# Cached pages of a paged latent attention: joined key and score products, value products turned round, rope scores in two row strips

## What is computed

```python
def mla_keys(c, w_uk, kn_g):
    return rms_norm(jnp.einsum('blc,chd->blhd', c, w_uk), kn_g)
def mla_scores(q_nope, q_rope, k_nope, kr):
    s = (jnp.einsum('bqhd,bkhd->bhqk', q_nope, k_nope) + jnp.einsum('bqhr,bkr->bhqk', q_rope, kr))
    return s * (MLA_QK ** -0.5)
# per page: c = lat_cache[layer, pages]; kr_p = kr_cache[layer, pages]
#   s = mla_scores(q_nope, q_rope, mla_keys(c, ...), kr_p)      8 heads x 8 queries per sample
#   p = exp(s - m);  l += sum(p);  acc += einsum('bhqk,bkc->bhqc', p, c)
# then the 8 new tokens themselves, and o = einsum('bhqc,chv->bqhv', acc / l, w_uv)
```

## Time and profile before

| what | us |
|---|---|
| three runs of the kernel | 1559.74, 1566.42, 1617.56 (median 1566.42) |
| the profiled execution | 1566.49 |
| its span, first to last instruction | 1564.8 |
| TensorE matmul busy in the span | 1498.6 (96%) |
| VectorE busy | 738.9 (47%) |
| ScalarE busy | 461.5 (29%) |
| GpSimd busy | 258.7 (17%) |
| granted TensorE clock, mean | 0.966 |

### The profile page before, as it was taken

One profiled execution on the slowest core, in us unless ns is written; L12 is line 12 of the kernel. 1 busy time (PEld: TensorE's weight loads), 2 busy tenths in 40 slices (PEclk: granted clock), 3 DMA queues, 4 the chain that ended last, 5 costly groups with the idle time before them and its releaser, 6 DMA issues.

```text
span 1564.8 us, 19947 instructions
## 1 busy us (share of the span) xinstructions
PE 1498.6 (96%) x6400; PEld 1039.4 (66%) x6400; DVE 738.9 (47%) x1446; ACT 461.5 (29%) x1013; POOL 258.7 (17%) x494
## 2 busy tenths in 40 slices
PE   7988889999998999999999888899999999999999
PEld 5656646666776777777766566566668667777776
DVE  1345658888514444430014466688883254444200
ACT  1236335545214111110012363454541141111100
POOL 2000244332022000001100002443320220000000
PEclk9999889999989999999999998899998899999999
DMA  6430424333035334333443204333320354333332
GB/s 247 121 98 0 186 87 120 105 93 104 1 121 167 121 122 123 122 103 123 149 134 112 82 33 170 96 116 100 106 75 28 118 170 121 121 124 122 113 111 94
DMA packets 83626, 174.46 MB, mean 111 GB/s; under 512 B 12641, under 2 KB 51074, under 8 KB 82626
## 3 DMA queue, kind: packets, MB, share of 16 engines
q1 hardware_dynamic: 73872, 163.55, 32.6%
q0 software_dynamic: 9504, 9.19, 2.0%
q10 hardware_dynamic: 146, 0.44, 0.1%
HBM read 166.84 MB, written 6.29 MB: 111 GB/s over the span
## 4 chain that ended last, share of the span: by engine, by line
PE 87%; DVE 7%; ACT 3%; issue 2%; POOL 1%; DMA 1%; SPq 0%; DVEq 0%
PE bank L444 35%; PE bank L786 14%; PE bank L1018 12%; PE bank L887 4%; PE bank L817 4%; PE bank L790 3%; PE bank L793 2%; PE bank L864 1%; ACT area L1574 1%; ACT area L1566 1%; PE bank L673 1%; PE bank L530 1%; POOL xg L1917 1%; PE bank L1003 1%; PE bank L479 1%
## 5 line engine op out<-in xcount | busy, mean ns | idle before, releaser
L444 PE MATMUL bank<-xg,slot 128*128 128x320 f32 x2048 | 558.6, 434 | 9.5 <-DMA slot<-in_weights 9.0
L444 PEld LDWEIGHTS bank<-xg,slot 128*128 128x128 f32 x2048 | 389.1, 190 | 174.4 <-DMA slot<-in_weights 9.0
L1782 ACT ACTIVATE sq<-bank 128x512 f32<-128x512 f32 x256 | 151.8, 593 | 172.4 <-PE bank L786 165.7
L1374 DVE TENSOR_REDUCE small<-sq 128x8 f32<-128x512 f32 x256 | 169.3, 682 | 63.4 <-ACT sq L1782 61.0
L1018 PE MATMUL bank<-area,slot 128*128 128x320 f32 x704 | 189.8, 432 | 0.0
L1018 PEld LDWEIGHTS bank<-area,slot 128*128 128x128 f32 x704 | 133.8, 190 | 55.7
L1930 POOL DMA_DIRECT2D krT<-in_cache_r x256 | 127.7, 499 | 226.9 <-issue 221.1
L1574 ACT ACTIVATE area<-area 128x336 f32<-128x336 f32 (+4 forms) x112 | 63.3, 567 | 334.1 <-DVE area L1523 300.8
L786 PE MATMUL bank<-wuk_nat,area 128*128 128x512 f32 x320 | 145.3, 597 | 0.0
L1466 DVE TENSOR_TENSOR x<-x,bank 128x320 f32<-128x320 f32 x48 | 23.4, 488 | 253.6 <-PE bank L1018 174.8
L1917 POOL TENSOR_SCALAR xg<-x,par 128x320 f32<-128x320 f32 x48 | 58.5, 1226 | 272.4 <-DVE x L1466 266.6
(11 more groups left out here) (324 smaller groups left out, 1746.8 us busy)
## 6 DMA issues: line engine op xcount, KB each, us to landing
slot<-in_weights SPq DMA_DIRECT2D x216, 512.0 KB, 3.6
area<-in_cache SPq DMA_DIRECT2D x160, 128.0 KB, 2.1
kept<-in_cache SPq DMA_DIRECT2D x96, 128.0 KB, 2.1
slot<-in_weights SPq DMA_DIRECT2D x18, 384.0 KB, 4.2
krT<-in_cache_r POOLq DMA_DIRECT2D x256, 16.0 KB, 2.0
xg<-in_ssd_t SPq DMA_DIRECT2D x2, 1024.0 KB, 4.7
area<-in_ssd_n SPq DMA_DIRECT2D x2, 1024.0 KB, 13.4
hs_out<-area POOLq DMA_DIRECT2D x2, 1024.0 KB, 4.1
```

The lines of the kernel that those rows point to most:

```text
L444: last = mm(out[:, 0:T], w[:, k, :], xg[:, k, :], start=(k == 0), stop=(k == KD - 1))
L1374: dve.tensor_reduce(ssk[:, t % 2, 8 * j:8 * j + 8], ksq[k % 3], AX.X, ALU.add).then_inc(V.fire(on["k_summed"]), 1)
L1782: f(ksq[k % 3], b[:, :].rearrange("p (h d) -> p h d", h=HEADS), ACT.Square).then_inc(A.free("key", l, t, j), 1)
```

## The change

- **Key and score products joined.** `wkq` holds, per head, 64 columns of the key weights with 8 query columns on each side, one side for even and one for odd samples. A page is multiplied with two halves of 4 heads x 72 columns (288 each), into two banks next to each other (`pair`, three pairs made of banks 0 to 5). A pair is freed by ScalarE's square. The separate score products are gone. GpSimd copies a sample's query columns into `wkq`.
- **Scores leave through ScalarE.** Per page ScalarE copies 64 columns into `score`, and per group 256 rope columns into `rope_sc`; VectorE then multiplies and adds in SBUF.
- **Rope scores in two strips.** Instead of one product with 128 rows and 256 columns there are two with 64 rows and 128 columns, one for each bank of the last page's pair.
- **Values turned round.** The probabilities are the weights (64 columns) and a page with a column of ones behind it moves through (129 columns). Even pages go to output rows 0 to 63, odd ones to 64 to 127. The column of ones gives the sum, so VectorE's sum and the product with ones are gone. ScalarE copies the result out (`cache_evict`), and TensorE adds the two halves and turns them back with two products of a folding matrix (`cache_fold`), one group later.
- **Rings.** What used the ring "mix" in this stage now uses the banks 6 and 7 ("late"). Behind the last group the prompt work waits until the last square is done, and one output tile of L864 is moved behind the last values.
- **Pages** are 260 numbers a row instead of 256. 

```diff
-PAGE_COLS = 2 * P
+PAGE_COLS = 2 * P + 4
...
-        self.t = [ctx.enter_context(nc.psum_tensor(f"bank{b}", [P, 512], F32)) for b in range(8)]
+        self.pair = [ctx.enter_context(nc.psum_tensor(f"pair{i}", [P, 1024], F32)) for i in range(3)]
+        self.t = [self.pair[b // 2][:, 512 * (b % 2):512 * (b % 2) + 512] for b in range(6)]
+        self.t += [ctx.enter_context(nc.psum_tensor(f"bank{b}", [P, 512], F32)) for b in (6, 7)]
...
-        wuk_nat = sb("wuk_nat", 512)
+        wkq = sb("wkq", 640)[:].rearrange("p (h c) -> p h c", h=HEADS)
...
+        rope_sc = [sq_t[:, 2048 + 256 * i:2304 + 256 * i] for i in range(2)]
+        pacc = [view(7778 + 132 * i, 132) for i in range(2)]
...
@@ TensorE: cache_group
-                for j in range(4):
-                    b = banks.open("proj", "key", l, t, j)
-                    pe.wait_ge(*banks.before("key", l, t, j))
-                    mm(b[:, :], pgroup[i][:, j, 0:P], wuk_nat[:, :], **F).then_inc(banks.full("key", l, t, j), 1)
-                b = banks.open("score", "sc", l, t)
-                pe.wait_ge(*banks.before("sc", l, t))
-                for j in range(4):
-                    mm(b[:, 64 * j:64 * j + 64], pgroup[i][:, j, 0:P], qt[:, :, NQ * s:NQ * s + NQ], **F)
-                n = l * NB * GROUPS + t
-                pe.wait_ge(krT_here[n % KR_GROUPS], 64 * (n // KR_GROUPS + 1))
-                mm(b[:, TP:2 * TP], krT[n % KR_GROUPS][:, :], qrep[:, :, :, NQ * s:NQ * s + NQ]
-                   .rearrange("p j h q -> p (j h) q"), **F).then_inc(banks.full("sc", l, t), 1)
+                at = 8 * (s % 2)
+                if g == 0:
+                    pe.wait_ge(*on["q_slot"].at(l, s + 1))
+                for j in range(4):
+                    k = 4 * t + j
+                    pair = banks.pair[k % 3]
+                    if k >= 3:
+                        pe.wait_ge(*on["key_free"].at(l, k - 2))
+                    else:
+                        pe.wait_ge(*banks.drained(2 * k))
+                        pe.wait_ge(*banks.drained(2 * k + 1))
+                    page = pgroup[i][:, j, 0:P]
+                    mm(pair[:, 0:288], page, wkq[:, 0:4, at:at + 72], **F)
+                    last = mm(pair[:, 512:800], page, wkq[:, 4:8, at:at + 72], **F)
+                    if j == 3:
+                        n = l * NB * GROUPS + t
+                        pe.wait_ge(krT_here[n % KR_GROUPS], 64 * (n // KR_GROUPS + 1))
+                        for half in range(2):
+                            rows = slice(64 * half, 64 * half + 64)
+                            last = mm(pair[:, 512 * half + 288:512 * half + 416], krT[n % KR_GROUPS][rows, :],
+                                      qrep[rows, 2 * half:2 * half + 2, :, NQ * s:NQ * s + NQ]
+                                      .rearrange("p j h q -> p (j h) q"), **F)
+                    last.then_inc(on["key_full"].sem, 1)
...
@@ TensorE: cache_values
-                for j in range(PAGES):
-                    i = (s * GROUPS + j // 4) % PGROUPS
-                    mm(b[:, 0:64], pgroup[i][:, j % 4, P:2 * P], prob[s % 2][:, j, :], start=(j == 0), stop=False)
-                mm(b[:, 0:64], c_tok[0:TS, 2, :], prob[s % 2][0:TS, PAGES, :], start=False, stop=True)
-                pe.wait_ge(*on["s_sum"].at(l, s + 1))
-                mm(b[:, 64:P], cc("ones"), sls, **F).then_inc(banks.full("pv", l, s), 1)
+                for j in range(STILES):
+                    i, r = (s * GROUPS + j // 4) % PGROUPS, 64 * (j % 2)
+                    tokens = pgroup[i][:, j % 4, P:2 * P + 1] if j < PAGES else c_new
+                    last = mm(b[r:r + 64, 0:P + 1], prob[s % 2][:, j, :], tokens, start=(j < 2), stop=(j >= PAGES - 1))
+                last.then_inc(banks.full("pv", l, s), 1)
+            def cache_fold(l, s):
+                pe.wait_ge(*banks.emptied("pv", l, s))
+                b = banks.open("late", "po", l, s)
+                pe.wait_ge(*banks.before("po", l, s))
+                mm(b[:, 0:64], pacc[s % 2][:, 0:P], cc("fold"), **F)
+                mm(b[:, 64:P], pacc[s % 2][:, P:P + 1].broadcast_to([P, P]), cc("fold"), **F).then_inc(banks.full("po", l, s), 1)
...
@@ TensorE: cache
                     if t == NB * GROUPS + 1:
+                        pe.wait_ge(*on["key_free"].at(l, NB * PAGES))
                         values_out_prompt(l)
...
-                    if t == NB * GROUPS + 5:
-                        for m in range(1, EARLY):
-                            mixed_out_prompt(l, m)
+                    if t in (NB * GROUPS + 5, NB * GROUPS + 6):
+                        mixed_out_prompt(l, t - NB * GROUPS - 4)
...
+                    if t % 4 == 2 and 0 <= t // 4 - 2:
+                        cache_fold(l, t // 4 - 2)
...
@@ VectorE: cache_scores
-                b = banks.of("sc", l, t)
-                dve.wait_ge(*banks.filled("sc", l, t))
                 out = score[s % 2][:, 4 * g:4 * g + 4, :]
-                TTO(out.rearrange("p t (h q) -> p (t h) q", h=HEADS),
-                    b[:, 0:256].rearrange("p (c q) -> p c q", q=NQ), spread(rsk[:, t % 2, :], 2, NQ),
-                    ALU.mult).then_inc(V.step(), 1)
-                dve.wait_ge(*V.last)
-                TTO(out, out, b[:, 256:512].rearrange("p (t c) -> p t c", t=4),
-                    ALU.add).then_inc(V.free("sc", l, t), 1)
+                flat = out.rearrange("p t (h q) -> p (t h) q", h=HEADS)
+                TTO(flat, flat, spread(rsk[:, t % 2, :], 2, NQ), ALU.mult).then_inc(V.step(), 1)
+                dve.wait_ge(*V.last)
+                TTO(out, out, rope_sc[t % 2].rearrange("p (t c) -> p t c", t=4), ALU.add).then_inc(V.fire(on["scored"]), 1)
...
@@ VectorE: removed
-            def cache_sum(l, s):
-                dve.wait_ge(*on["s_exp"].at(l, s + 1))
-                dve.tensor_reduce(sls, prob[s % 2].rearrange("p t c -> p c t"), AX.X, ALU.add).then_inc(V.fire(on["s_sum"]), 1)
...
@@ ScalarE: cache_group
-                        b = banks.of("key", l, t, j)
-                        act.wait_ge(*banks.filled("key", l, t, j))
-                        act.wait_ge(*on["k_summed"].at(l, 1 + max(0, k - 2)))
-                        f(ksq[k % 3], b[:, :].rearrange("p (h d) -> p h d", h=HEADS),
-                          ACT.Square).then_inc(A.free("key", l, t, j), 1)
+                    if s >= 2 and k % PAGES == 0:
+                        act.wait_ge(*on["s_exp"].at(l, s - 1))
+                    act.wait_ge(*on["key_full"].at(l, k + 1))
+                    b = banks.pair[k % 3][:].rearrange("p (a c) -> p a c", a=2)
+                    b4 = b[:, :, 0:288].rearrange("p a (h c) -> p a h c", h=4)
+                    copy(score[s % 2][:, k % PAGES, :].rearrange("p (a h q) -> p a h q", a=2, h=4),
+                         b4[:, :, :, 64 * (s % 2):64 * (s % 2) + NQ]).then_inc(A.step(), 1)
+                    if j == 3:
+                        if t >= 2:
+                            act.wait_ge(*on["scored"].at(l, t - 1))
+                        copy(rope_sc[t % 2].rearrange("p (a c) -> p a c", a=2), b[:, :, 288:416]).then_inc(A.step(), 1)
+                    act.wait_ge(*on["k_summed"].at(l, 1 + max(0, k - 2)))
+                    f(ksq[k % 3].rearrange("p (a h) d -> p a h d", a=2), b4[:, :, :, NQ - at:NQ - at + 64],
+                      ACT.Square).then_inc(A.fire(on["key_free"]), 1)
+                    if t % 4 == 2 and j == 1 and 0 <= t // 4 - 2:
+                        cache_evict(l, t // 4 - 2)
...
+            def cache_evict(l, s):
+                b = banks.of("pv", l, s)
+                act.wait_ge(*banks.filled("pv", l, s))
+                copy(pacc[s % 2][:, 0:P + 1], b[:, 0:P + 1]).then_inc(A.free("pv", l, s), 1)
...
@@ GpSimd
+            def query_slot(l, s):
+                if s >= 2:
+                    pool.wait_ge(*on["key_full"].at(l, PAGES * (s - 1)))
+                pool.wait_ge(*G.last)
+                at = 72 * (s % 2)
+                pool.tensor_copy(wkq[:, :, at:at + NQ], qt[:, :, NQ * s:NQ * s + NQ]).then_inc(G.fire(on["q_slot"]), 1)
```

More of the change, by code:

```diff
@@ L65 @@
           ("causal", 384), ("cos", T), ("sin", T), ("hmask", 4), ("bmask", NB), ("pmask", 4),
-          ("invn", 1), ("eps", 1)]
+          ("invn", 1), ("eps", 1), ("fold", 64)]
 def columns(table):
@@ L155, in emptied, with drained @@
         return self.bank_free[b], n
+    def drained(self, b):
+        return self.bank_free[b], self.count[b]
 class Lane:
@@ L537, in new_scores @@
                 pe.wait_ge(*banks.before("new_key", l))
-                mm(b[0:TS, 0:512], ckvn[:, TP:T], wuk_nat[:, :], **F).then_inc(banks.full("new_key", l), 1)
+                mm(b[0:TS, 0:512], ckvn[:, TP:T], wkq[:, :, 8:72], **F).then_inc(banks.full("new_key", l), 1)
                 b = banks.open("mix", "new_nope", l)
@@ L1372, in key_sum @@
                 k = 4 * t + j
-                dve.wait_ge(*banks.emptied("key", l, t, j))
+                dve.wait_ge(*on["key_free"].at(l, k + 1))
```

(25 more changed lines are left out.)

56 lines of the change are left out of this document (29 added, 27 removed).

## The result

The changed kernel takes 1516.91 us (median of four runs, 1515.71 to 1518.27) where the kernel before, on the same chip, took 1568.77 (median of four). One of these four, 1617.56, fell in a slower state and is left out of the ratio, which is 0.9688 with a 95% interval of 0.9643 to 0.9733. The forecast was 1529 with a range of 1512 to 1556, so the time lies within the range and 12 us under the forecast. Those 12 us are what has to be explained. The profiled execution took 1517.22 us, its span is 1515.6.

What follows compares the result with a forecast made beforehand. The prediction took TensorE, busy 96% of the span, to bound the kernel. From 1566.5 us it took 33.4 for two layers' stage and 4 for the clock behind it: 1529 us, range 1512 to 1556.

Steps and rivals of the forecast that it cites:

- Group: TensorE's group of four pages: 4.41 us instead of 4.75, from 3.86 for key and scores plus 0.55 for rope.
- Values: Value products in two column tiles side by side: 2.35 us plus fold 0.45 against 4.25, saving 1.45 a sample.
- The wait before the transpose: TensorE waits 0.5 us for the maximum in seven of eight samples, 3.5 us a layer lost.
- ScalarE and VectorE: Both engines in the stage: 18.2 and 17.7 of some 21.7 us a sample, so neither binds as a sum.
- bank loop: Key and score bank pairs freed by ScalarE's square: a page's slack remains, at most 0.1 us lost there.
- Sum of the stage: Cached stage per layer: groups 9.8, values 11.6, waits -3.5, end -1.2, together 16.7 us saved; two layers 33.4.
- The clock behind the stage: Half-speed clock behind the cached stage in both layers: falls later or shorter, 4 us gained (0 to 15).
- rival 3: The clock stays up behind the stage: 11 us more gained, 1518 us; chance 11%.
- main sum: Whole kernel: 1566.5 less 33.4 for the stage and 4 for the clock, 1529 us (1515 to 1541); chance 50%.
- Rival 1: Hand-overs in the three-pair bank loop bind harder: 1.3 us more a sample, 21 us, 1550 us; chance 22%.
- Rival 2: Rope strips run in turn (0.78 us): 1541 us; if the values' tiles did too, 1569; chance 11%.
- Rival 4: Slower: the clock falls within the stage, at a fifth of it 1598 us; chance 6%.

Runs made afterwards that it cites:

- one-tile run: Changed kernel with all 17 value products in one column tile (output rows 0 to 63), fold on 64 rows: 1547.96 us, ratio 0.9873.
- values first: Changed kernel with a sample's values issued ahead of the transpose of the next sample's maximum: 1509.60 us, ratio 0.9648; measured again 1509.36 us.
- full rope product: Changed kernel with both rope products on all 128 rows instead of strips: 1522.39 us, ratio 0.9731; with values first added, 1505.71 us, ratio 0.9614.
- full broadcast: Values first with full rope product, plus the broadcast of the maximum (L831) made a 128-row product by rows of zeros: 1507.40 us, ratio 0.9620.

## Why the prediction was right, and where it was off

The steps in the order in which the prediction makes them, with the stretches of the profiled execution:

- **Group.** 4.41 forecast, 4.50 measured from key product to key product. The key and score part is right (0.485 for two passes against 0.482). The rope step is 0.62, not 0.55. The prediction had 0.33 around two steps of 0.112 (way in, weight load, exit); measured are 0.10 ahead of the strips, 0.42 for the strips, and 0.10 in the next group's first key pair (0.59 instead of 0.49), so 0.40 around the two steps. It is inside the bounds of 0.42 to 0.78, and the strips do run side by side: four passes end 0.49 us after the first one's start, four full ones after 0.61. In two of four groups a product that isn't of the full shape follows anyway (transpose or broadcast) and the exit is shared; over a sample the miss is nearly nil.
- **The rule of the Trainium skill** ("TensorEngine Tiling (Array Packing)", "Key Properties") that a change of mode drains the engine: the traces agree in that a change of shape costs time on both sides, 0.2 us in all; that a drain is the reason they do not show. Without the drain the prediction put 0.3 us a group; the strips cost 0.17 more than the full product at an undisturbed boundary.
- **Values.** 2.35 forecast, 2.12 measured; fold 0.45 and 0.50. Together 1.63 us a sample saved where 1.45 was forecast, and the one-tile run shows that the tiles are the cause.
- **The wait before the transpose.** 0.5 forecast, 0.37 measured, in the samples forecast, put down to the maximum as forecast. The maximum was ready 4.82 us after its group's last rope product (4.91 forecast), and the group that runs meanwhile is 0.09 longer than forecast. The run with the values first shows that it cost TensorE its full length. The prediction said that behind it waits only TensorE's own queue. It did not see that this queue could be turned round.
- **ScalarE and VectorE.** The 128x64 copy takes 0.22 (0.23 forecast), and VectorE is busy 126.42 of 155.00 us from 225 to 380, 82% (80% forecast). The bank loop costs the matmuls nothing here; it begins to bind only when the group gets shorter, as the full rope product showed (0.17 a sample). ScalarE was busy 108.13 of 155.00 us, 70%; the forecast's 84% added full durations, which overlap.
- **Sum of the stage.** By stretches of the stage in layer 0, gains forecast and measured: first nine groups 1.5 and 1.15 (45.11 to 43.96), group 9 to the last 13.2 and 14.93 (134.41 to 119.48), end 2.0 and 1.89 (30.31 to 28.42). Together 16.7 and 17.97. The first groups bound to the loads' pace and the end went as charged. 33.4 forecast for two layers, 35.8 measured.
- **The clock behind the stage: the term that was mis-sized.** The prediction says "All 30 us at full speed would give back 15; I take 4 (0 to 15)". It gave 16.2. That is outside the term's own bounds. The direction was right, and the cause was named right (the 256-column tile now stands between the values and the new tokens' output). But the reasoning that the fall would only come later took the 64-column passes that follow for enough to bring it. They were not, in this kernel: 28.5 us of them ran at 1.00 in both layers, also with the old stage in front (the tile alone). What stands ahead of them matters: with the tile taken back the clock fell in both layers again. (The fall before began when TensorE had done 64-column passes for 4.3 us, not 5, and stood in the pause behind them.) This was rival 3, given 11% and 1518 us; with 1516.9 it is the case that came true, and the range held the time because it took most of it in. That the number lies in the range is in this part luck: the main sum, 1529, did not come true. That the kernel would be faster did not hang on it: without the 12.2 us it would still be 2.4% under the time before.
- **Outside** nothing was charged, and 2.9 us were lost: from the end of layer 0's output to layer 1's stage it is 530.5 us instead of 528.5, and behind layer 1's output 326.8 instead of 325.1, with a stretch at clock 0.92; ahead of layer 0's stage 0.9 was gained. Why the 2.0 were lost is not shown.

```profile
1203.00:1218.00 15.00, 13.90 (x133) 9.23 (x131) 8.03 (x20) 9.71 (x34) 0.28 (x2) 0.92 0.48 159
```

Rival 1 (hand-overs bind harder) did not come: no wait beyond the forecast one. Rival 2 (strips or tiles in turn) is refuted by both timelines; the one-tile run is what it would have looked like for the values, 1548 us. Rival 4 did not come either: clock 1.00 in both stages, although TensorE was idle 8.4 and 7.4 us in them.

Taken apart, the profiled 49.2 us are 35.8 from the stage and 16.2 from the clock behind it, less 2.9 elsewhere. What the moved tile has of this depends on what it is compared with. Taken back out of the changed kernel it costs 14.0 (13.2 by the clock, 0.9 by the cover of ScalarE's copy); moved alone in the kernel before it gives 17.8 between the medians, where the fall was deeper and the tile also covered VectorE's division. In the changed kernel that division is not covered:

```profile
410.23 0.43 PE L905 MATMUL bank<-olat,slot 128*128 128x64 f32 x2 [0.98 <-DVE olat L1449]
```

## What to carry to other kernels

Price what stands ahead of a stretch of narrow products: one wide tile moved between two stretches of narrow products gave about a third of this change (14 to 18 us), nearly all of it by the clock, and could be had alone. When a bound engine waits once per round for a result, look in its own queue for work that doesn't need it; here the values did not, and swapping two calls took 10 us out of the two stages. And a product of another shape costs at its borders, so count borders and not products: here strips next to another 64-row product cost no border of their own ahead of it, and removing them alone gained nothing until the last 64-row product was gone too.

## What the hardware showed that was not expected

- **The same code kept the clock in one layer and lost it in the other.** With the values first, the same instructions run behind the stage in both layers. Layer 0 took 28.51 us at clock 1.00, layer 1 35.10 at 0.81:

```profile
1146.39:1181.49 35.10, 35.10 (x144) 28.05 (x145) 5.86 (x12) 3.68 (x8) 8.97 (x7) 0.81 0.38 120
```

  The second execution of the same kernel did the same (28.52 and 35.11), and so did the one with the full rope product (28.52 and 35.09). The kernel with the full broadcast stayed at 28.52 in both layers, and the one-tile kernel fell in layer 0 and not in layer 1. The Trainium skill ("TensorE: Matmul & The Clock Gate", "Part 1: The HAM clock gate") says that the activity check runs free of the program, so that the point of a change moves from run to run. That leaves room for layers that differ under the same code, but these traces do not confirm it: all three profiled executions with the values first and a 64-row broadcast fell in layer 1 and none in layer 0, which points to something ahead of the stretch rather than to chance, but no run tests it. Counted over the profiled executions, two layers each: with the tile behind the last values the clock stayed up in 14 layers of 18, without it in none of 4. What decides within the 18 is not settled here. Such a fall costs 6.6 us (8.0 and 8.2 in the kernel before), so a kernel can lose by it what it gained in the stage.
- **A change of shape costs on both sides**: 0.10 us on the way into 64 rows (the pass behind a key pair starts after 0.58 instead of 0.49) and 0.10 in the first key pair behind it.
- **Column tiles of 64 run side by side**: 0.057 us a pass for 129 columns in two tiles, 0.112 in one.
- **ScalarE's small copies overlap**: a 128x64 copy lasts 0.22 us, and the next instruction starts 0.12 us after the copy's start.

```profile
318.85 0.22 ACT L1588 ACTIVATE xg<-pair 128x64 f32<-128x64 f32 x1 [0.78 <-PE pair L808]
318.97 0.59 ACT L1814 ACTIVATE sq<-pair 128x512 f32<-128x512 f32 x1
```
